# Merge-gate columns taken out of the input projection and multiplied in float32 beside attention and the two preparation stages

## The reference, cut to what matters

```
P = split_in(h @ w_in)                 # gdn, na, hg, rw ... 8016 columns, then 'merge' 4096
y_a, y_b, y_c, y_d = ...               # DeltaNet, neighbourhood attention, HGRN2, RWKV-7
gates = sigmoid(P['merge']).reshape(B, L, 4, 1024)
proj  = einsum('blmc,mcd->blmd', branches, w_branch)
out   = sum(gates * proj, axis=2) @ w_out
```

## Time and profile before

| | us |
|---|---|
| runs shown (three) | 10385.37, 10404.98, 10477.92 |
| their median | 10404.98 |
| the profiled execution's own time | 10368.56 |
| its span, first to last instruction | 10366.7 |
| PE, DVE, POOL, ACT busy | 7257.5, 5139.0, 4216.7, 1738.7 |

### The profile page before, as it was taken

One profiled execution on the slowest core, in us unless ns is written; L12 is line 12 of the kernel. 1 busy time (PEld: TensorE's weight loads), 2 busy tenths in 40 slices (PEclk: granted clock), 3 DMA queues, 4 the chain that ended last, 5 costly groups with the idle time before them and its releaser, 6 DMA issues. The chain is left out here.

```text
span 10366.7 us, 85981 instructions
## 1 busy us (share of the span) xinstructions
PE 7257.5 (70%) x31402; PEld 4773.7 (46%) x31402; DVE 5139.0 (50%) x7657; ACT 1738.7 (17%) x3172; POOL 4216.7 (41%) x2958
## 2 busy tenths in 40 slices
PE   6998378178685377777769983781886754777676
PEld 2886268078634122222238862780785341222222
DVE  3332566622235866664533325666222357656644
ACT  0002233222110011111100022332221100111111
POOL 1330312233101777777713303122331017777776
PEclk8996589578797799999979965895887877999999
DMA  4331220410222899999943312104003229999999
GB/s 161 128 118 50 78 77 21 160 40 29 83 105 94 315 375 384 380 375 403 389 161 119 118 50 86 69 27 165 29 29 115 100 74 347 383 368 381 372 407 369
DMA packets 610672, 1952.58 MB, mean 188 GB/s; under 512 B 69429, under 2 KB 87221, under 8 KB 604473
## 3 DMA queue, kind: packets, MB, share of 16 engines
q0 software_dynamic: 368640, 1342.34, 33.8%
q1 hardware_dynamic: 241642, 605.09, 16.0%
HBM read 1803.46 MB, written 150.05 MB: 188 GB/s over the span
## 5 line engine op out<-in xcount | busy, mean ns | idle before, releaser
L615 PE MATMUL expert_acc<-expert_row,expert_diag 128*128 128x512 f32 x4864 | 2411.8, 624 | 1146.9 <-DMA expert_row<-in_peer_v,expert_idx 750.4
L733 DVE CUSTOM_DVE_ANT_0 expert_junk<-expert_row,expert_h 128x1024 f32<-128x1024 f32 x1280 | 1560.4, 1226 | 1205.2 <-DMA expert_row<-in_peer_u,expert_idx 1171.4
L615 PEld LDWEIGHTS expert_acc<-expert_row,expert_diag 128*128 128x128 f32 x4864 | 855.7, 194 | 2697.9 <-issue 1325.2
L582 POOL DMA_INDIRECT expert_row<-in_peer_u,expert_idx x1280 | 1394.5, 1089 | 661.8 <-issue 389.7
L582 POOL DMA_INDIRECT expert_row<-in_peer_v,expert_idx x1280 | 1387.8, 1084 | 390.3 <-issue 236.6
L334 POOL TENSOR_TENSOR proj_wl<-proj_w,proj_wh 128x4096 fp32r<-128x4096 f32 (+1 forms) x56 | 499.7, 8924 | 2225.0 <-DVE proj_wh L382 2225.0
L311 PE MATMUL proj_ps<-proj_wl,proj_hT 128*128 128x512 f32 (+1 forms) x2240 | 883.1, 394 | 97.3 <-POOL proj_wl L334 97.3
L311 PE MATMUL proj_ps<-proj_wh,proj_hT 128*128 128x512 f32 (+1 forms) x2240 | 882.1, 394 | 0.0
L311 PE MATMUL proj_ps<-proj_wh,proj_hTl 128*128 128x512 f32 (+1 forms) x2240 | 881.9, 394 | 0.0
L649 ACT ACTIVATE expert_diag<-expert_ident,expert_wt 128x128 f32<-128x128 f32 x1216 | 472.6, 399 | 2346.0 <-PE expert_acc L615 2269.4
L1794 POOL TENSOR_TENSOR scan_kl<-scan_hkT,scan_ex 128x1024 f32<-128x1024 f32 x70 | 179.7, 2567 | 831.4 <-ACT scan_ex L1759 831.4
(11 more groups left out here) (451 smaller groups left out, 11106.4 us busy)
## 6 DMA issues: line engine op xcount, KB each, us to landing
proj_w<-in_w_in SPq DMA_DIRECT2D x46, 2048.0 KB, 9.8
mod_w<-in_w_mod SPq DMA_DIRECT2D x24, 2048.0 KB, 7.6
scratch_PR<-proj_o SPq DMA_DIRECT2D x46, 1024.0 KB, 5.3
rprep_xs<-scratch_PR SPq DMA_DIRECT2D x30, 928.0 KB, 12.5
gprep_xs<-scratch_PR SPq DMA_DIRECT2D x30, 768.0 KB, 7.8
scratch_RQ<-rprep_res SPq DMA_DIRECT2D x10, 2304.0 KB, 7.6
merge_gates<-scratch_PR SPq DMA_DIRECT2D x10, 2048.0 KB, 7.5
expert_row<-in_peer_u,expert_idx POOLq DMA_INDIRECT x1280, 6.5
```

What stands on the lines that cost most here:

```text
L582: pool.indirect_dma_start(out=slot(kind, n), out_offset=None, in_=e.peer_u if kind == "dot" else e.peer_v, in_offset=bass.IndirectOffsetOn ...
L615: mm = pe.matmul(acc[:, i % 2, c, :], diag[:, done % DIAGS, :], slot("sum", n)[:, c * CHUNK:(c + 1) * CHUNK], start=(k == 0), stop=(k == P ...
L733: dve.tensor_tensor_reduce(junk[:, n % 2], slot("dot", n), h[:, i % 2], 1.0, 0.0, ALU.mult, ALU.add, hid[:, k:k + 1]).then_inc(s.dot, 1)
```

## The change

What it does:

- `project_stage` is called with the first 8016 columns, which are 16 chunks (15 of 512 and one of 336) in place of 24. At its end DVE adds the high and low parts of hT into a float32 copy `keep`, which lies where the input x was and lives on past the stage.
- A new class `MergeColumns` holds two weight buffers of 256 columns, two result buffers, one PSUM bank, and the semaphores. The 4096 merge columns are 16 chunks of 256, and a chunk times a token tile is one filler: 8 float32 matmuls of 256 columns into the one bank (`multiply`), read out by ACT (`read_out`). 80 fillers a layer: 40 in attention (one a unit), 25 in `gdn_prepare` (five a tile), 15 in `rwkv_prepare` (three a tile). A filler waits for the read-out of the one before.
- In attention the filler stands between the transposes of the probabilities and the wait for ACT's copy of them, ACT's read-out at the end of its unit. To free a PSUM bank, the result `po` goes from two banks to one, and the bias table's matmuls write to `ps`.
- SP's queue loads the first two chunks of merge weights ahead of attention's own loads, and stores and loads between the others.
- `rwkv_prepare` moves from `rwkv_pass` to right behind `gdn_prepare`, ahead of the scans. Two more stages are closed each layer.

The diff, cut to its core:

```diff
-def project_stage(nc, e, l, part, w_src, n_cols, dst_lat, dst_ctx):
+def project_stage(nc, e, l, part, w_src, n_cols, dst_lat, dst_ctx, keep=None):
...
-        x = st.sb("x", [P, TILES, D])
+        x = st.sb("x", [P, TILES, D]) if keep is None else keep
...
                 in_pairs(dve, split_high)
+                if keep is not None:
+                    step(dve.tensor_tensor(keep.rearrange("p m d -> p (m d)").rearrange("p (k t) -> p k t", k=KD), hT[:],
+                                           hT_low[:], ALU.add))
                 read_out(dve, dve.tensor_copy, 1, s_v, n_pairs - 1, 1, sizes[-1], False)
...
+class MergeColumns:
+    W = 256
+    FIRST = COL['merge']
+    COUNT = 4 * D // W * TILES
+    def load(self, sp, c):
+        if c >= 2:
+            sp.wait_ge(self.s_mm, TILES * (c - 1))
+        c0 = self.FIRST + c * self.W
+        sp.dma_start(self.w[:, c % 2], self.e.w_in[self.l][:, c0:c0 + self.W].rearrange("(k p) n -> p k n", p=P))\
+          .then_inc(self.s_w[c % 2], 16)
+    def store(self, sp, c):
+        PR, c0 = self.e.PR, self.FIRST + c * self.W
+        cols = slice(c0, c0 + self.W)
+        sp.wait_ge(self.s_kept, TILES * (c + 1))
...
+    def multiply(self, pe, f):
+        c, m = f // TILES, f % TILES
+        if m == 0:
+            pe.wait_ge(self.s_w[c % 2], 16 * (c // 2 + 1))
+        if f:
+            pe.wait_ge(self.s_kept, f)
+        for k in range(KD):
+            mm = pe.matmul(self.ps[:, 0:self.W], self.hT[:, k, m * P:(m + 1) * P], self.w[:, c % 2, k, :],
+                           start=(k == 0), stop=(k == KD - 1))
+        mm.then_inc(self.s_mm, 1)
+    def read_out(self, act, f):
+        c, m = f // TILES, f % TILES
+        act.wait_ge(self.s_mm, f + 1)
+        if m == 0 and c >= 2:
+            act.wait_ge(self.s_out[c % 2], 32 * (c // 2))
+        act.copy(self.o[:, c % 2, m, :], self.ps[:, 0:self.W]).then_inc(self.s_kept, 1)
...
+NA_FILL, GDN_FILL, RWKV_FILL = 8 * TILES, 5 * TILES, 3 * TILES
...
 # attention_stage
-        ps, pt, po = st.ps("ps", [P, 2, 2, CHUNK]), st.ps("pt", [P, 2, CHUNK]), st.ps("po", [P, 2, CHUNK])
+        ps, pt = st.ps("ps", [P, 2, 2, CHUNK]), st.ps("pt", [P, 2, CHUNK])
+        po = st.ps("po", [P, CHUNK])
...
             def _(sp):
+                mc.load(sp, 0)
+                mc.load(sp, 1)
                 sp.wait_ge(s_one, 1)
...
                     tr.then_inc(s_p, 1)
+                    mc.multiply(pe, u)
                     pe.wait_ge(s_pc, u + 1)
-                    if u >= 2:
-                        pe.wait_ge(s_y, u - 1)
+                    if u >= 1:
+                        pe.wait_ge(s_y, u)
...
                     copy_probs(u)
+                    mc.read_out(act, u)
...
 # gdn_prepare
+            @block.tensor
+            def _(pe):
+                for f in range(GDN_FILL):
+                    mc.multiply(pe, NA_FILL + f)
...
                     act.activation(sig[:], xs3[:, m % 3, 0, :], ACT.Sigmoid).then_inc(s.sig, 1)
+                    for f in range(2):
+                        mc.read_out(act, NA_FILL + TILES * m + f)
                     act.wait_ge(s.ss, m + 1)
                     act.activation(ss2[:, m % 2, 2, :], ss2[:, m % 2, 1, :], ACT.Sqrt).then_inc(s.root, 1)
+                    for f in range(2, TILES):
+                        mc.read_out(act, NA_FILL + TILES * m + f)
...
 # rwkv_prepare
                 first(0)
                 for m in range(TILES):
+                    for f in range(RWKV_FILL // TILES):
+                        mc.read_out(act, NA_FILL + GDN_FILL + RWKV_FILL // TILES * m + f)
                     if m + 1 < TILES:
                         first(m + 1)
                     second_half(m)
...
                     pe.matmul(ps[:, 3, :], loraT[:, 1, :], g2[:], start=True, stop=True).then_inc(s.mm, 1)
+                    for f in range(RWKV_FILL // TILES):
+                        mc.multiply(pe, NA_FILL + GDN_FILL + RWKV_FILL // TILES * m + f)
...
 # build
-            project_stage(nc, e, l, 0, e.w_in[l], IN_W, e.PR[ROW_LAT:ROW_LAT + LAT, :], e.PR[ROW_CTX:ROW_CTX + CTX, :])
-            attention_stage(nc, e, l)
+            with Stage(nc, "hidden") as held:
+                hT = held.sb("hT", [P, TILES, D])
+                project_stage(nc, e, l, 0, e.w_in[l], COL['merge'], e.PR[ROW_LAT:ROW_LAT + LAT, :],
+                              e.PR[ROW_CTX:ROW_CTX + CTX, :], keep=hT[:])
+                with Stage(nc, "mcols") as st:
+                    mc = MergeColumns(st, e, l, hT[:])
+                    attention_stage(nc, e, l, mc)
+                    gdn_prepare(nc, e, l, mc)
+                    rwkv_prepare(nc, e, l, mc)
```

More of the change, by code:

```diff
@@ L212, in _ @@
                 ins.then_inc(s_scaled, 1)
-def project_stage(nc, e, l, part, w_src, n_cols, dst_lat, dst_ctx):
+def project_stage(nc, e, l, part, w_src, n_cols, dst_lat, dst_ctx, keep=None):
     sizes = [CHUNK] * (n_cols // CHUNK) + ([n_cols % CHUNK] if n_cols % CHUNK else [])
+    if len(sizes) % 2:
+        sizes[-1:] = [sizes[-1] // 2] * 2
+    starts = [sum(sizes[:j]) for j in range(len(sizes))]
     n = len(sizes)
@@ L946, in attention_stage @@
+NA_FILL, GDN_FILL, RWKV_FILL = 8 * TILES, 5 * TILES, 3 * TILES
+def attention_stage(nc, e, l, mc):
     B, RB = 4, 15
@@ L988, in _ @@
                         e.PR[ROW_CTX:ROW_CTX + CTX, c0:c0 + 512].rearrange("j (h d) -> j h d", h=NA_H))
-                for n, m in enumerate(list(range(1, TILES)) + [0]):
-                    sp.wait_ge(s_y, NA_H * (n + 1))
-                    out(e.Y[m * P:(m + 1) * P, 512:1024], y[:, m, :])
+                order = list(range(1, TILES)) + [0]
+                for u in range(len(units)):
+                    if u % TILES == TILES - 1:
+                        c = u // TILES
+                        mc.store(sp, c)
+                        mc.load(sp, c + 2)
+                    if u % NA_H == NA_H - 1:
+                        m = order[u // NA_H]
+                        sp.wait_ge(s_y, u + 1)
+                        out(e.Y[m * P:(m + 1) * P, 512:1024], y[:, m, :])
                 out.wait()
@@ L1002, in _ @@
                         ck = 4 * n + c
-                        mm = pe.matmul(po[:, n % 2, c * 120:(c + 1) * 120], shift[:, ck * P:(ck + 1) * P], rpb[:],
+                        mm = pe.matmul(ps[:, n % 2, 0, c * 120:(c + 1) * 120], shift[:, ck * P:(ck + 1) * P], rpb[:],
                                        start=True, stop=True)
@@ L1016, in _ @@
                 pe.wait_ge(s_tc, len(groups))
+                pe.wait_ge(s_blo, NT)
+                pe.wait_ge(s_bhi, NT)
                 def scores(u):
@@ L1046, in values @@
                             (vc[:, h * NA_D:(h + 1) * NA_D] if m else x[:, 0, 1024 + h * NA_D:1024 + (h + 1) * NA_D])
-                        mm = pe.matmul(po[:, u % 2, 0:NA_D], pT[:, u % 2, b * P:(b + 1) * P], v,
+                        mm = pe.matmul(po[:, 0:NA_D], pT[:, u % 2, b * P:(b + 1) * P], v,
                                        start=(b == blocks[0]), stop=(b == 4))
@@ L1163, in first_row, with gdn_prepare @@
     return ROW_CTX if m == 0 else ROW_LAT + (m - 1) * P
-def gdn_prepare(nc, e, l):
+def gdn_prepare(nc, e, l, mc):
     W, QK = 1536, 1024
@@ L1212, in _ @@
                         load(m + 3)
+                    c = NA_FILL // TILES + m
+                    mc.store(sp, c)
+                    mc.load(sp, c + 2)
                 sp.wait_ge(s.q, 2)
@@ L1951, in scan_pass @@
 def scan_pass(nc, e, l):
-    gdn_prepare(nc, e, l)
     scan_stage(nc, e, l)
@@ L1960, with rwkv_prepare @@
 RQ = {name: 512 * n for n, name in enumerate(RQ_PARTS)}
-def rwkv_prepare(nc, e, l):
+def rwkv_prepare(nc, e, l, mc):
     with Stage(nc, "rprep") as st:
@@ L2017, in _ @@
                         load(m + 3)
+                    c = (NA_FILL + GDN_FILL) // TILES + m - 1
+                    if 1 <= m <= RWKV_FILL // TILES:
+                        mc.store(sp, c)
+                        if (c + 2) * TILES < mc.COUNT:
+                            mc.load(sp, c + 2)
+                mc.stored(sp)
                 for b in range(2):
@@ L2427, in rwkv_pass @@
 def rwkv_pass(nc, e, l):
-    rwkv_prepare(nc, e, l)
     with Stage(nc, "rres") as st:
```

23 lines of the change are left out of this document (18 added, 5 removed).

## The result

The changed kernel takes 10105.72 us (median of 4 runs, 10094.44 to 10117.53); beside it the kernel before took 10413.44 (10385.37 to 10477.92). The ratio is 0.970, with a 95% interval of 0.965 to 0.974. The forecast was 10120, in a range of 10030 to 10250. The medians are 308 us apart, where the sum had said 282 and the forecast, against the 10404.98 known then, 285. The profiled executions stand at 10096.36 and 10368.56, 272 us apart.

The account below looks back on a forecast made before the run. PE was taken to bound the projection at 2.4 GHz and attention at 1.2 GHz, with PE nearly free in both preparations. Terms summed to -141 us a layer, -282 in all, giving 10087 to 10123; forecast 10120, range 10030 to 10250.

Parts of the forecast that it names:

- the sum: All stages: -223 + 22 + 22 + 35 + 3 = -141 us a layer, -282 in all.
- Removed: Projection: 8 chunks fewer, each 120 matmuls and 27.9 us of PE, -223 us a layer.
- Price of a filler: A filler's 8 float32 matmuls are 16 passes: 3.45 us at full clock, 6.9 us at 1.2 GHz.
- The clock: Attention: fillers of 128-row work without a pause raise PE's clock, full from the second unit on.
- Attention: Attention stage: latent units -9, context units +21, start +7 and a cold first filler +3, together +22 us a layer.
- the cold filler: Attention's start: the first filler runs before the clock has risen, +3 us (0 to 7).
- `gdn_prepare`: This preparation stage: second and fourth tiles lengthen, +13; stage end +6.5; weight traffic +2; sum +22 us a layer.
- The ring: `rwkv_prepare`: each tile's products, ACT's stretch, a table load and fillers follow in turn, 29 us a tile; stage +35 us.
- A: Rival: clock stays at 1.2 GHz in attention and both preparations; +197 us a layer, 10800 us; chance 6%.
- B: Rival: full clock in attention only, pauses keep it down in the preparations; -44 us in all, 10360 us; chance 6%.
- C: Rival: the preparations' tiles realign and cover nearly all fillers, attention's units take 6.4 us; 10035 us; chance 10%.
- D: Rival: the projection does not shorten by 8 chunks because something else sets its end; no number; chance 1%.

Follow-up runs that it names:

- with two banks: The changed kernel with fillers taking turns in two PSUM banks in the two preparation stages: 10061.36 us in one run.
- half-filler kernel: The changed kernel with 4 of each filler's 8 matmuls, merge gates incomplete: 9918.12 us in one run.
- 64-row run: The changed kernel with each filler's matmuls on 64 of 128 rows, merge gates incomplete: 10820.69 us, ratio 1.040.
- the kernel's second run: The changed kernel once more, without any edit: 10095.5 us, ratio 0.971.
- 10021 by placement: The changed kernel with read-outs dealt out anew in both preparation stages and attention's first merge weights loaded behind its own loads: 10021.13 us, ratio 0.961.

## Why the prediction was right, point by point

**Removed.** -223 a layer forecast, -222 and -224 measured. PE alone set the projection's end, and 120 matmuls a chunk at the spacing of the earlier trace rows were the whole working.

**Price of a filler.** 3.45 us forecast. In the units a filler takes 3.46 (800.57 to 804.03), and with two banks they follow one another at 3.45. The 512-column row of another stage was the right row to halve.

**The clock.** Forecast: 1.2 GHz at first, then full from the second unit. The first filler took 5.8 us (700.93 to 706.73), the second 3.46; the granted clock was 1.00 during the last transposes of q and k and the first scores (692.0 to 698.5 us), 0.50 from 699.0 to 705.5, behind a wait of 2.68 us for ACT, and 1.00 from 706 us on. The Trainium skill ("TensorE: Matmul & The Clock Gate", PE-mode transpose) states that transposes don't count for the gate as other work does. This trace doesn't agree, nor do: in both kernels the clock rose during the transposes of q and k, which begin at 686.2 here and at 902.3 before (rise at 692.0 and 907.6), behind 27.7 us of 32-row products at half clock and ahead of any filler. The half-filler kernel decides nothing here, since each of its units has 1.7 us of filler and some 1.2 of products with v, all on 128 rows. The 64-row run adds that with PE always busy, the filler's rows alone made the difference between 0.50 and 1.00.

**Attention.** +22 forecast, +24 and +22.5 measured, but with a different make-up. The first 30 steps from unit to unit went from 6.87 us each to 9.35 once and 6.49 then: -8.5, with the cold filler in it (forecast -9 and +3). The other nine steps gave +19.0 (forecast +21 for the eight context units, which take 4.64 instead of 2.17). The bias table's products start 14.2 us into the stage instead of 9.2: +5.0 (forecast 7). What I had not priced is the stage's end: "what SP's wait for the fillers holds back is needed by nobody in the stage" is wrong for the last unit. SP in the changed kernel:

```profile
945.22 0.33 SPq L975 DMA_DIRECT2D scratch_PR<-mcols_o  x1
945.59 0.44 SPq L976 DMA_DIRECT2D scratch_PR<-mcols_o  x1
946.21 0.43 SPq L968 DMA_DIRECT2D mcols_w<-in_w_in  x1
946.68 1.16 SPq L103 DMA_DIRECT2D scratch_Y<-na_y  x1
955.36 0.81 SPq L1270 DMA_DIRECT2D gprep_xs<-scratch_PR  x2
```

and in the kernel before:

```profile
1148.31 0.32 SPq L103 DMA_DIRECT2D scratch_Y<-na_y  x1
1152.37 0.80 SPq L1193 DMA_DIRECT2D gprep_xs<-scratch_PR  x2
```

The last store of y is issued behind a chunk's stores and a load of 1 MB, and the stage ends 8.7 us after its issue instead of 4.1. From the last transposes to the stage's end it is 14.4 us instead of 6.0: +8.4, of which some 3.5 are the last unit's own filler. It was offset by the start, the context units and the latent units, each some 2 us cheaper than said: the sum came out close with one term missing.

**`gdn_prepare`.** +22 forecast, +18 measured. ACT's sigmoids and its last read-out, after:

```profile
988.96 1.48 ACT L1341 ACTIVATE gprep_sig<-gprep_xs 128x1536 f32<-128x1536 f32 x1 [9.82 <-DVE gprep_xs L1365]
...
1017.54 1.48 ACT L1341 ACTIVATE gprep_sig<-gprep_xs 128x1536 f32<-128x1536 f32 x1 [5.78 <-DVE gprep_xs L1365]
...
1039.01 1.48 ACT L1341 ACTIVATE gprep_sig<-gprep_xs 128x1536 f32<-128x1536 f32 x1
...
1064.04 1.48 ACT L1341 ACTIVATE gprep_sig<-gprep_xs 128x1536 f32<-128x1536 f32 x1 [4.07 <-DVE gprep_xs L1365]
...
1083.83 1.48 ACT L1341 ACTIVATE gprep_sig<-gprep_xs 128x1536 f32<-128x1536 f32 x1
...
1103.11 0.37 ACT L995 COPY mcols_o<-mcols_ps 128x256 f32<-128x256 f32 x1 [3.81 <-PE mcols_ps L986]
```

The gaps are 28.6, 21.5, 25.0 and 19.8, against 28.5, 17.1, 29.2 and 14.0. The second and fourth tiles have the 22 us of the forecast (21.5 and 19.8), ACT coming to these sigmoids without a wait for DVE. Two terms were off, with opposite signs. The third gap, which I had left at 29.2, gave 4 us back: from the second sigmoid to the fourth it is 46.5 us, before 46.3, so the lateness of the third was absorbed, and the gaps give +6 in all where the sum had +13. (In the kernel's second run this gap was 21.0.) The stage's end gives +11 where the sum had +6.5: it comes 29.2 us after the fifth sigmoid instead of 18.0. ACT's last read-out is 19.3 us after it, as said, but then the stage's last store goes out behind a chunk's stores and load, as in attention, and the stage ends 8.1 us after its issue instead of 5.5.

**`rwkv_prepare`.** +35 forecast, +29 measured. ACT's read-outs and the start of the next tile, after:

```profile
1223.22 0.37 ACT L995 COPY mcols_o<-mcols_ps 128x256 f32<-128x256 f32 x1 [10.82 <-PE mcols_ps L986]
1227.40 0.37 ACT L995 COPY mcols_o<-mcols_ps 128x256 f32<-128x256 f32 x1 [3.81 <-PE mcols_ps L986]
1231.59 0.37 ACT L995 COPY mcols_o<-mcols_ps 128x256 f32<-128x256 f32 x1 [3.81 <-PE mcols_ps L986]
1231.86 0.31 ACT L2130 ACTIVATE rprep_lora<-rprep_xs 128x128 f32<-128x128 f32 x1
```

The ring is the one that the prediction drew, with 27.4 us a tile instead of 29: ACT goes into the next tile 0.27 us after its last read-out. The first filler of a tile took 5.1 (1218.09 to the read-out at 1223.22) where the sum had 6.0 for it. In the time of the earlier trace rows DVE's last step ends at 2097, where the sum had 2101. The other two small terms were nearly nothing: the +3 for loads came to 0.4 at the first tile's transposes, and of the +3 for two more exits 0.9 shows, from DVE's last step to the next stage (10.6 instead of 9.7).

**Rivals.** A fell in the changed kernel and held in the 64-row run, where its condition was made true. B fell in its price: +18 and +29 where it had +99 and +77. Its mechanism was there in part, with a clock of 0.86 and 0.73 in the preparations, but only the first filler behind a pause was slow. C (10035) isn't what the changed kernel did, but its condition, tiles that cover the fillers, can be made: 10021 by placement, and 9945 with more of the fillers in the preparations. D fell with the projection's 512 us.

## What to carry to other kernels

Work moved onto a busy TensorE can cost less than its own time when it raises the granted clock: price it with rows at both levels, and try the work that you add on all rows of the array, as here, where 64 rows were not enough. Such filler is then limited by its read-outs and by the queue that feeds it: put a read-out where its engine has slack by the timeline, and issue a filler's load ahead of waits for the host stage's steps, not behind, but keep it from standing ahead of the host stage's last store. Where a stage seems full, look for a wait on a transfer first.

## What the runs showed of the hardware that was not expected

With PE busy for 180 of 180 us the granted clock was 0.50 with fillers on 64 rows and 1.00 with as many matmuls a unit on 128 rows. The other products of the unit were the same in both.

The clock fell again in short stretches without filler: the first filler after a tile's pause took 6.2 us in `gdn_prepare` (28.5 us without a matmul before it), 5.4 there after 5.0 us without one, and 5.0 to 5.3 in `rwkv_prepare`, where it follows 5.5 us of cold products; the fillers right behind them took 3.7.

```profile
990.75 6.19 PE L986 MATMUL mcols_ps<-mcols_w,hidden_hT 128*128 128x256 f32 x16 [28.49 <-ACT mcols_o L995]
997.41 3.72 PE L986 MATMUL mcols_ps<-mcols_w,hidden_hT 128*128 128x256 f32 x16 [0.46 <-ACT mcols_o L995]
```
